# Retention's values projected by tokens in front of the retention heads, and a quarter of the attention branch's gated projection behind each head

## The reference

```
h = rms_norm(x);  z = h @ w_in                      # columns: retention q,k,v,g; spatial u,v; attention q,k,v; gates
ya = retention(rotary(qa), rotary(ka), va)          # 4 heads of 128, decay per head
ya = silu(ga) * rms_normalize(ya) * ret_norm_g
yb = gelu(ub) * (tril(w_s) @ layer_norm(gelu(vb)) + b)
yc = attention over 3 dilation groups x 4 heads, joined by their softmax denominators
x = x + (sum_b sigmoid(gate_b) * (y_b @ w_branch[b])) @ w_o
h = rms_norm(x);  x = x + (silu(h @ w_gate) * (h @ w_up)) @ w_down
```

## Time and profile before

| | |
|---|---|
| median of 3 runs | 1910.8 us (1909.89 to 1911.27) |
| the profiled execution | 1910.71 us, of which the span is 1908.9 us |
| PE busy | 1894.6 us, 99% of the span |
| DVE busy | 1246.4 us, 65% |
| ACT busy | 844.4 us, 44% |
| POOL busy | 96.9 us, 5% |
| HBM | 194 GB/s over the span |

### The profile page before, as it was taken

The page is one execution under the profiler, slowest core; times in us unless marked ns, Lnnn a source line. Parts: engine busy times, 40 slices in busy tenths (PEclk is TensorE's granted clock), DMA queues, the critical chain, the costliest instruction groups (busy, mean ns, idle before and its releaser), DMA issues. The chain is left out here.

```text
span 1908.9 us, 26594 instructions
## 1 busy us (share of the span) xinstructions
PE 1894.6 (99%) x10632; PEld 1699.3 (89%) x10632; DVE 1246.4 (65%) x1625; ACT 844.4 (44%) x1186; POOL 96.9 (5%) x148
## 2 busy tenths in 40 slices
PE   8999999999999999999999999999999999999999
PEld 7888888888888899899888888888888888998998
DVE  7767767746566786377576667677365657863775
ACT  5544444524234464155335444345242344642554
POOL 0000001111111000000000000011111110000000
PEclk9999999999999999999999999999999999999999
DMA  5322356787777355366333222577777773653663
GB/s 203 95 78 67 89 135 182 190 221 206 205 204 207 93 177 173 100 191 198 120 100 95 67 78 83 144 199 185 210 211 211 194 201 92 193 159 107 201 210 122
DMA packets 85897, 295.68 MB, mean 155 GB/s; under 512 B 20368, under 2 KB 20624, under 8 KB 84624
## 3 DMA queue, kind: packets, MB, share of 16 engines
q1 hardware_dynamic: 73104, 218.49, 36.8%
q0 software_dynamic: 12672, 75.51, 17.1%
HBM read 291.79 MB, written 77.66 MB: 194 GB/s over the span
## 5 line engine op out<-in xcount | busy, mean ns | idle before, releaser
L1057 ACT ACTIVATE w_high<-raw 128x1024 fp32r<-128x1024 f32 x396 | 418.3, 1057 | 791.7 <-PE bank L847 663.1
L1266 DVE TENSOR_TENSOR w_low<-raw,w_high 128x1024 fp32r<-128x1024 f32 x396 | 483.0, 1222 | 147.6 <-ACT w_high L1057 141.0
L847 PE MATMUL bank<-h_high,w_high 128*128 128x512 f32 x1408 | 543.5, 386 | 8.9 <-DVE h_low L1271 8.2
L847 PE MATMUL bank<-h_low,w_high 128*128 128x512 f32 x1408 | 534.3, 379 | 0.0
L847 PE MATMUL bank<-h_high,w_low 128*128 128x512 f32 x1408 | 534.1, 379 | 0.0
L847 PEld LDWEIGHTS bank<-h_high,w_high 128*128 128x128 f32 x1408 | 266.7, 189 | 47.0 <-issue 8.1
L847 PEld LDWEIGHTS bank<-h_high,w_low 128*128 128x128 f32 x1408 | 266.6, 189 | 38.0
L847 PEld LDWEIGHTS bank<-h_low,w_high 128*128 128x128 f32 x1408 | 266.8, 189 | 36.2
L847 PE MATMUL bank<-in_high,w_high 128*128 128x512 f32 x672 | 255.0, 379 | 0.0
L847 PE MATMUL bank<-in_low,w_high 128*128 128x512 f32 x672 | 254.7, 379 | 0.0
L847 PE MATMUL bank<-in_high,w_low 128*128 128x512 f32 x672 | 254.7, 379 | 0.0
(11 more groups left out here) (163 smaller groups left out, 2344.3 us busy)
## 6 DMA issues: line engine op xcount, KB each, us to landing
raw<-weights SPq DMA_DIRECT2D x325, 512.0 KB, 4.1
weight_sums<-weights POOLq DMA_DIRECT2D x108, 512.0 KB, 6.1
raw<-weight_sums SPq DMA_DIRECT2D x72, 512.0 KB, 3.8
weight_sums<-weight_sums POOLq DMA_DIRECT2D x36, 512.0 KB, 4.1
turned<-rows SPq DMA_DIRECT2D x3, 768.0 KB, 6.8
xT<-x_t SPq DMA_DIRECT2D x8, 256.0 KB, 5.4
decay_sb<-decay SPq DMA_DIRECT2D x8, 256.0 KB, 5.0
out_t<-xT SPq DMA_DIRECT2D x8, 256.0 KB, 6.4
```

The lines of the kernel that those rows point to most:

```text
L847: return pe.matmul(o, w, m, start=start, stop=stop)
L1057: act.activation(w_high[:, PART_SLOT[s], :, :], raw[:, s % RAW_SLOTS, :, :], ACT.Copy).then_inc(part_high_w.sem, 1)
L1266: dve.tensor_tensor(w_low[:, PART_SLOT[s], :, :], raw[:, s % RAW_SLOTS, :, :], w_high[:, PART_SLOT[s], :, :], ALU.subtract).then_inc(part_ ...
```

## The change

Retention's values of all four heads are projected as `sv` is, with tokens on the partitions, in four tiles `("rv", 0)` to `("rv", 3)` in front of the first `rq`. Their four banks are `stat_bank`, `out_bank`, the first score bank, and the main bank that the last attention value tile has just used; ACT copies them to SBUF once after the fourth tile. The four transposes of each head, its scaling on DVE and its copy on ACT are gone. A head now has the tiles `rq`, `rk`, `rg`, then two gates and two products of `gated(2)`. The slots of the small steps in a head are still counted from its `rq`.

```diff
@@ tiles_of_layer
-    for h in range(HEADS):
-        t += [("rq", h), ("rk", h), ("rv", h), ("rg", h)]
-
-    def gated(branch):
+    t += [("rv", j) for j in range(HEADS)]
+
+    def gated(branch, pairs=range(KT // 2)):
         out = []
-        for n in range(0, KT, 2):
+        for n in pairs:
+            n *= 2
             out += [("gate", branch, n), ("gate", branch, n + 1), ("proj", branch, n), ("proj", branch, n + 1)]
         return out
-    t += gated(2)
+    for h in range(HEADS):
+        t += [("rq", h), ("rk", h), ("rg", h)] + gated(2, [h])
@@ schedule
         post[t + 1] += [("rotate", "rk", h)]
-        pre[t + 3] += [("vtrans", "rv", h)]
         pre[t + 3] += [("rscore", h, m) for m in range(2)]
         pre[t + 4] += [("rscore", h, m) for m in range(2, BLK)]
         pre[t + 6] += [("rpv", h), ("ocopy", h), ("square", "r", h), ("split_sq", "r", h)]
@@ build
-        token_bank = score_bank + [out_bank, stat_bank]
+        def token_bank(base, role):
+            if role == "sv":
+                return score_bank + [stat_bank, out_bank]
+            return [stat_bank, out_bank, score_bank[0], bank_of(base, AT["rv", 0] - 1)]
@@ gpsimd
-                pool.wait_ge(tile_stored.sem, tile_stored.at(layer * STRIDE, AT["rv", 0]))
+                pool.wait_ge(tile_stored.sem, tile_stored.at(layer * STRIDE, AT["rq", 0]))
@@ tensor, by_token
-                if j == 0:
-                    pe.wait_ge(ret_copied.sem, ret_copied.at(base, HEADS - 1))
+                if role == "sv" and j == 0:
                     pe.wait_ge(std_ready.sem, std_ready.at(base, "cq", HEADS - 1))
+                if role == "rv" and j == 0:
+                    pe.wait_ge(low_ready.sem, low_ready.at(base, "yc", HEADS - 2))
+                    pe.wait_ge(std_ready.sem, std_ready.at(base, "cq", HEADS - 1))
+                    pe.wait_ge(score_taken.sem, score_taken.at(base, "scores", HEADS - 1, 2))
@@ tensor, by_token, in front of the three matmuls of block b
+                        if role == "rv" and k == 0 and b == BLK - 1:
+                            wait_evacuated(pe, base, i - 1)
+                        if role == "sv" and k == 0 and b == BLK - 1:
+                            pe.wait_ge(ret_copied.sem, ret_copied.at(base, HEADS - 1))
@@ scalar, token_evac
+                        for b in range(BLK):
+                            dst, func = (ret_v[b], ACT.Copy) if role == "rv" else (sg_v[:, b, :], ACT.Gelu_apprx_tanh)
+                            act.activation(dst, token_bank(base, role)[b][:, :], func, scale=rs[:, b:b + 1]).then_inc(
+                                values_ready.sem, 1)
```

More of the change, by code:

```diff
@@ L151 @@
     PROJECTION_EVENTS += [("slab", b[0]) for b in _bs[:-1] if LAST_BLOCK[b[0]] == (_i, b)] + [(_i,)]
-SCALED_ROLES = {"rq", "rk", "v", "rv", "rg", "su", "gate", "fgate"}
+TOKEN_ROLES = ("rv", "sv")
+SCALED_ROLES = {"rq", "rk", "v", "rg", "su", "gate", "fgate"}
 ACTIVATED_ROLES = {"rg", "su", "gate", "fgate"}
@@ L307, in schedule @@
             steps.append(("main", i, 0, len(BLOCKS[i])))
-        steps += splits + pre[i] + ([("evac", i)] if TILES[i][0] != "sv" else [("token_evac",)] if i == AT["sv", HEADS - 1] else [])
+        steps += splits + pre[i] + ([("evac", i)] if TILES[i][0] not in TOKEN_ROLES else
+                                [("token_evac", TILES[i][0])] if TILES[i][1] == HEADS - 1 else [])
         steps += later + post[i]
@@ L393, in build @@
         input_sum = over("input_sum", in_low_at + 4 * row_bytes, [P, 2, 4, 2 * P], F32)
+        ret_v_rows = [over("values_high", in_high_at + 10 * row_bytes, [P, 2, SEQ], F32),
+                      over("values_low", in_low_at + 10 * row_bytes, [P, 2, SEQ], F32)]
+        ret_v = [ret_v_rows[m // 2][:, m % 2, :] for m in range(BLK)]
         work_at = nc.sbuf_base
@@ L461, in build @@
         row_sq = [in_high[:, 8:10, :], in_low[:, 8:10, :]]
-        ret_std, k_std2 = work[:, 16, :], work[:, 17, :]
+        ret_std, k_std2 = work[:, 7, :], work[:, 17, :]
         ssq = work[:, 12, :]
@@ L524, in build @@
         ret_copied = signal("ret_copied", keys("ocopy"))
-        values_ready = signal("spatial_values_ready", [(b,) for b in range(BLK)])
+        values_ready = signal("values_ready", [(role, b) for role in TOKEN_ROLES for b in range(BLK)])
         ln_var = signal("ln_var_ready", [()])
@@ L889, in main @@
             def main(base, i, first, end):
-                if TILES[i][0] == "sv":
+                if TILES[i][0] in TOKEN_ROLES:
                     by_token(base, i, TILES[i][1])
                     return
-                if i >= 2 * AHEAD_OF_NORM and first == 0:
+                if i == AT["rq", 0]:
+                    wait_evacuated(pe, base, AT["rv", 0] - 2)
+                elif i == AT["rk", 0]:
+                    pe.wait_ge(values_ready.sem, values_ready.at(base, "rv", BLK - 1))
+                elif i >= 2 * AHEAD_OF_NORM and first == 0:
                     wait_evacuated(pe, base, i - (4 if i < 3 * AHEAD_OF_NORM else
@@ L1026, in _ @@
                             pe.wait_ge(ret_copied.sem, ret_copied.at(base, h - 1))
[L1027 removed]
+                        if h == 0:
+                            pe.wait_ge(values_ready.sem, values_ready.at(base, "rv", BLK - 1))
                         for m in range(BLK):
                             pe.wait_ge(score_taken.sem, score_taken.at(base, "rscore", h, m))
[L1030 removed]
+                            last = matmul(out_bank[:, m * P:SEQ], ret_v[m][:, h * P:(h + 1) * P], ret_s[:, RS_OFF[m]:RS_OFF[m] + SEQ - m * P],
                                           m == 0, m == BLK - 1)
@@ L1647, in _weights @@
                 src, col, row0 = w_down[layer], t[2] * P, t[1] * FF_BLOCKS[0] * P
-            elif t[0] == "sv":
+            elif t[0] in TOKEN_ROLES:
                 for s, place, i in blocks:
                     k, at = 2 * t[1] + i // 4, i % 4 * P
-                    values = w_in[layer][k * P:(k + 1) * P, of(("sv", 0)):of(("sv", 0)) + HEADS * P]
+                    values = w_in[layer][k * P:(k + 1) * P, of((t[0], 0)):of((t[0], 0)) + HEADS * P]
                     values = values.reshape(P, 2 * P, 2).transpose(0, 2, 1).reshape(P, HEADS * P)
```

36 lines of the change are left out of this document (14 added, 22 removed).

## The result

The changed kernel takes 1916.49 us (median of 7 runs, 1915.96 to 1917.66), against 1910.89 for the kernel before in the same comparison (7 runs, 1909.75 to 1911.59). The ratio is 1.0033, with a 95% interval of 1.0023 to 1.0042: slower by 5.6 us. The forecast was 1918.5, which is +7.8. Of all executions in this document one was slow, 3348.51 us at a granted clock of 0.556, of the kernel with DVE's scaling a slot later; ratios leave it out.

The account below looks back on a forecast made before the run. PE bounds the kernel: its own instructions plus its waits, each new wait counting in full. Terms -3.5 - 1.0 - 0.8 + 3.4 + 9.7 = +7.8 on 1910.7 gave 1918.5 us, +0.4%; 8-in-10 range 1912 to 1922.5.

Parts of the forecast that it names:

- The rotation of `rk`: At the scores of heads 1 to 3, both layers, PE waits for DVE's second rotation: 6 x 1.62 = +9.7 us.
- lateness plus 0.34: Price of a PE wait: its lateness plus 0.34 us for the signal and refilled pipeline; bounds 0.15 and 0.34.
- The wait in the first value tile: PE's tenth matmul there waits for DVE to scale the fourth bank: 1.8 and 1.6 us, +3.4; bounds 3.0 and 4.0.
- falls into the same 1.8: First value tile: the other new wait, for scores DVE reads earlier, was not added to the fourth bank's 1.8 us.
- The transposes: Eight groups of four PE transposes, four heads in two layers, go at 0.43 to 0.44 us each: -3.5 us.
- the waits that go: Old PE waits vanish: head 3's row sums, -1.0 us; head 0's value transposes in layer two, -0.8 us.
- It adds nothing: Second gate, behind the scores: its bank needs DVE's scaling of `rg`, 0.68 us beside two scores, so no extra wait.
- The table load: ACT's load before the root counted as 1.28 us by trace; the skill's 2.66 would add an estimated 8.3 us.
- POOL's later start: POOL's weight sums start two tiles, some 10 us, later; costed at nothing, with 35 us of cover.
- A: Rival: `rk`'s rotation is done when PE comes, needing DVE's chain 1.28 us shorter; 1908.8 us, -0.1%; chance 0.10.
- B: Rival: all new waits are covered and only what is removed counts; 1905.4 us, -0.3%; chance 0.04.
- C: Rival: ACT reaches the root later, through one more table load or a late copy; 7.7 us more, 1926; chance 0.06.

## Why the prediction came out right, and what in it did not

**What bounds the kernel** held. The result is PE's instructions plus PE's waits, and the table of start times adds up to the difference of the medians.

**The rotation of `rk`** (+9.7 forecast, +8.56 measured) was right in mechanism, place and count; the experiments with the scaling moved and the row lengthened show the cause by both signs. The end of the row on DVE was right to 0.04. Mis-sized was the term "lateness plus 0.34": 1.28 + 0.34 = 1.62 forecast. Measured at head 1 are 1.24 + 0.14 for the signal (332.31 - 332.17) + 0.08 for the restart = 1.46, at the other five 1.20 + 0.15 + 0.07 = 1.42. So the price was 0.22, between the forecast's bounds of 0.15 and 0.34. The 0.34 came from the earlier trace rows, where a restart of 0.19 shows over the row sums and the plain matmuls behind them; in front of the scores it was less than half of that, and why was not tried. This term is 1.1 of the 2.2 us by which the forecast was high.

**The wait in the first value tile** (+3.4 forecast, +2.65 measured) was right in place, but it is two waits, and the step "falls into the same 1.8" was right in that they share one lateness. What failed is the size: 1.42 and 1.23 instead of 1.8 and 1.6, and 2.65 lies below the lower bound of 3.0. DVE's scaling of the permuted tile, 1.52 in the earlier trace rows, takes 1.34 now (1.42 in layer two, against 1.55), and the signal to PE took 0.05. This is 0.75 of the 2.2.

**The transposes** (-3.5) and **the waits that go** (-1.8 forecast, -2.07 measured): the row sums went as forecast. The wait of 0.80 in layer two went whole; the probabilities did not inherit any of it. In layer one I had overlooked a shorter one at the same place of the kernel before:

```profile
267.64 0.38 PE L847 MATMUL bank<-h_high,w_low 128*128 128x512 f32 x1
268.08 0.63 PE L977 MATMUL bank<-identity,scaled 128*128 128x128 f32 x4
```

0.44 in place of 0.22; with the slower restart of the transposes 0.27, the last part of the 2.2. All three misses made the forecast too high, so none of them hid another. The 0.80 is not in every execution of such a schedule: in the two kernels of the experiments that keep the transposes this gap is 0.44 in both layers. So up to 0.5 of the 2.07 may be chance.

**"It adds nothing"**, said of the second gate's bank, was true of the changed kernel and misleading beyond it. The scaling of `rg` lay beside the scores, 332.77 against 333.60, and only because PE ran them just then. I did not carry that over when I moved the scores, and two experiments came out 12 us off. Moving the one that waits is no cure when the next instruction waits for the same row.

**The table load.** The root starts 0.01 behind the load's end:

```profile
315.21 1.06 ACT L1074 ACTIVATE w_high<-raw 128x1024 fp32r<-128x1024 f32 x1 [3.40 <-PE bank L849]
316.29 1.28 ACT L1189 ACT_TABLE_LOAD   x1
317.58 0.69 ACT L1189 ACTIVATE work<-bank,eps 128x512 f32<-128x512 f32 x1
```

The Trainium skill (ScalarE: Activation LUTs, section What ACT_TABLE_LOAD costs) gives some 1380 ns of drain beside the load. The trace has neither behind the load nor ahead of it (0.02 after the split) any room for that, so the sum was right to go by the trace. In the kernel without the load the root ended 1.42 earlier, the load and 0.14, where load and drain would be 2.66.

**POOL's later start**: a further 40 us made no difference, so the two tiles of the change, some 10 us, are not behind the loss.

**Rivals.** A (the rotation in time) did not come. Its condition was about right, for the rotation was 1.20 to 1.24 late, but the table load would not have met it: without the load the wait still stands at 0.56, since DVE's own weight split then holds the inversion. B, only the removals count, did not come either. The changed kernel with one number of its schedule and the block order of one tile put right is what it describes: 4.4 faster than its own runs of the kernel before, where the removals came to 5.6, which lies within the interval. The profiled spans differ by 5.1, and 0.5 more lies ahead of the edited stages, where executions differ anyway: PE comes to the last attention scores of layer one at 245.42 there and at 244.91 in the kernel before. C, an additional load in the chain, did not come: the root stood where the rows of before put it.

So the change saves 5.6 us on PE by what it removes, and loses 11.2 by the waits that its order brings.

## What to carry to other kernels

When a change shortens the group of tiles between two fixed slots, list in order what the slower engine does between the slots, add it up, and compare with the tiles that PE has left; here 17.4 against 16.2 us decided it, though DVE was busy for only 65% of the span. If the row is too long, take out of it what nobody waits for soon (here the head's own scaling), rather than move the instruction that waits: the next one waits for the same row. And price a wait as lateness, plus the signal, 0.05 to 0.15 us here, plus the restart, which was 0.07 to 0.10 at most places and 0.19 at the row sums.

## What the hardware showed unexpectedly

The same DVE instruction on the same bank, the permuted scaling, took 1.52 and 1.55 us in the kernel before and 1.34 and 1.42 in the changed one. There PE stood still for a part of it. The other kernels bear this out. With only the block order of that tile changed, PE does not stop there, and the scaling takes 1.52 and 1.55 again; so it does, within 0.01, in all kernels without that wait of PE, and 1.33 to 1.34 and 1.41 to 1.42 in all that have it. So this instruction takes longer where PE's matmuls run on through it; why is not shown by any run. The kernel before could not show it, and this is part of why the forecast of that term was too high.

In the kernel with the longer row one of the six waits, of the same 2.1 us as the others, was followed by slow matmuls. PE, and windows of the same stretch (busy time of each engine, granted clock, DMA share, GB/s):

```profile
1359.36 0.38 PE L849 MATMUL bank<-h_high,w_low 128*128 128x512 f32 x1
1361.72 2.16 PE L849 MATMUL bank<-work 128*128 128x512 f32 x4 [1.98 <-DVE work L1465]
1363.10 1.20 PE L849 MATMUL bank<-h_high,w_high 128*128 128x512 f32 x1
1364.10 0.63 PE L849 MATMUL bank<-h_low,w_high 128*128 128x512 f32 x1
...
1359.00:1363.00 4.00, 2.02 (x7) 0.98 (x6) 3.94 (x6) 2.01 (x3) 0.60 (x1) 0.99 0.40 131
1363.00:1366.00 3.00, 3.00 (x8) 2.22 (x7) 2.99 (x5) 2.69 (x3) 0.20 (x1) 0.50 0.75 124
```

For 3 us the granted clock was 0.50, that is 1.2 GHz; the matmuls started 0.43 apart instead of 0.216, some 1.7 us lost by the starts. Before the fall PE had stood for 2.1 us. The other five waits of that length show no such fall, nor do the six of about 2 in the kernel with the scores later, nor those of 1.4 in the changed kernel. So a wait of about 2 us can cost nearly double; why this one did is open. It was seen in one profiled execution; whether the other three of that kernel (1921.01 to 1924.76) had one isn't known.
